# The slots of two weight rings moved from 8192 to 8208 bytes apart

## The chip, the cores and the metric

The kernel runs on one core of one Trainium2 chip. The metric is the device time of one execution in microseconds (us). Three runs of the kernel before gave 1250.34, 1250.72 and 1251.28 us; the median is 1250.72 us.

## What is computed

The reference is one transformer stack in float32 on 256 tokens of width 1024: first two layers (a gated delta-rule mixer with 8 heads, then block attention with 8 heads, each followed by a squared-ReLU MLP of width 4096), then a third layer with four parallel branches (differential attention, forgetting attention, a 31-tap convolution, a short convolution), a gated sum of them, cross attention to 256 memory tokens and a gated feed-forward of width 2816. For this case only one thing matters: nearly all of the work is a product of activations with a weight matrix that is read once from memory.

```python
h = h + squared_relu_mlp(rmsnorm(h, mlp_norm_g[i]), mlp_w_up[i], mlp_w_down[i])
def squared_relu_mlp(hn, w_up, w_down):
    return jnp.square(jax.nn.relu(hn @ w_up)) @ w_down
```

## The kernel before

The weights come in units of 1 MB: 128 partitions by 2048 float32, so 8192 bytes in each partition. SyncE starts one DMA for each unit into one of the two slots of `raw` (line 285). ScalarE rounds the unit into a slot of the ring `whi` (line 297: the high part, type fp32r), and VectorE writes what the rounding left into the same slot of the ring `wlo` (line 305: raw minus high). Both rings have four slots (`RING = 4`), and unit U lies in slot U mod 4. The splits run three units ahead of the product (`AHEAD = 3`).

TensorE then multiplies. The activations are split the same way: `xparts` holds the high and low halves of the 256 normed tokens (turned, 8 pieces of 256 columns each), `hhi` and `hlo` the hidden values of an MLP, `bhi` and `blo` the outputs of attention and of the branches. Every product is high*high + high*low + low*high, so a weight tile is used by three matmuls (`mm3`, lines 369, 372 and 373). There are four forms of it:

- features (line 426 on): the weights are the stationary operand, tiles of 128x128 of `whi` or `wlo`; `xparts` or `bhi`/`blo` stream past, 256 columns. 48 matmuls for each unit.
- tokens (line 577 on): activations are stationary, `whi` or `wlo` streams, 256 columns. 48 matmuls.
- rows (line 592 on): `hhi`/`hlo` (or `bhi`/`blo`, or `xparts`) are stationary, `whi` or `wlo` streams, 512 columns. 24 matmuls; the down projections.
- wide (line 441 on): `wlo` is stationary and the high half of `xparts` streams, 256 columns (line 450), then `whi` is stationary and both halves of `xparts` stream in one matmul of 512 columns (line 454). 32 matmuls; the up projections of the MLPs.

Each matmul has its own load of the stationary operand (PEld in the profile), which runs while the matmul before it streams. So at every moment TensorE reads two things from the memory on the chip: the moving operand of one matmul and the stationary operand of the next, and of the two one lies in a ring of weights and the other in a buffer of activations.

Buffers stand in a partition in the order in which `build` makes them (lines 167 to 199): `raw` (16384 bytes), `whi` (32768), `wlo` (32768), `xparts` (16384), `hhi` and `hlo` (4096 each), `h`, `gain` (8192 each), `smr`, `ident`, `ones` (512 each), `row_of` (64), `staged_rows`, `row_parts` (1024 each), `upper` (512), `masks` (3072), `dn_lower` (512), `smo` (256), `sm` (1024), `common` (39392), `head_rows`, `dn_x` (2048 each), and then `bhi` and `blo` (16384 each), over the place of `dn_extra`, which is given back before. All of them up to `common` are multiples of 64 bytes; `common` is not (39392 = 615 * 64 + 32). So seen from the start of any slot of `whi` or `wlo`, `xparts`, `hhi` and `hlo` lie at a whole number of 64 bytes, and `bhi` and `blo` lie 32 bytes past one (from `whi`: 159008 = 2484 * 64 + 32).

Of the kernel before, what the change touches and what calls it, by code (L numbers as in the profile page):

```python
# [22 lines left out]
F32R = mybir.dt.float32r  # L23
# [5 lines left out]
P = 128  # L29
# [4 lines left out]
RING = 4  # L34
RAW = 2
AHEAD = 3
UNIT = 2048
# [119 lines left out]
def build(nc, A, out):  # L157
    ctx = ExitStack()
    with ctx:
        def sb(name, shape, dt=F32, c=ctx):  # L160
            return c.enter_context(nc.sbuf_tensor(name, shape, dt))
# [3 lines left out]


        raw = sb("raw", [P, RAW, UNIT])
        whi = sb("whi", [P, RING, UNIT], F32R)
        wlo = sb("wlo", [P, RING, UNIT], F32R)
        xparts = sb("xparts", [P, 2, KT, T], F32R)  # L170
        xhi, xlo = xparts[:, 0], xparts[:, 1]
        hhi = sb("hhi", [P, 2, 2, T], F32R)
# [3453 lines left out]
```

## Time and profile before

| | |
|---|---|
| median of 3 runs | 1250.72 us |
| span of the profiled execution | 1249.1 us |
| granted TensorE clock over the span | 0.998 of 2.4 GHz |
| PE busy | 1220.7 us (98%) |
| PEld busy | 1106.9 us (89%) |
| DVE busy | 871.6 us (70%) |
| ACT busy | 700.5 us (56%) |
| weights split (L297, L305) | 190 units each |

The span runs from the first to the last instruction of the profiled execution; it is 1.6 us shorter than the median of the timed runs. PE is TensorE's matmuls, PEld its loads of the stationary operand, DVE VectorE, ACT ScalarE. Matmuls are pipelined and overlap in the records, so what one costs in a long sequence is not its duration but its pitch: the distance from its start to the start of the next.

### The profile page before, as it was taken

What the parts mean: (1) busy time and instruction counts of PE and PEld (TensorE: products, weight loads), DVE (VectorE), ACT (ScalarE), POOL (GpSimd) and SP (SyncE); (2) the same over time, 40 slices, a digit from 0 to 9 for tenths busy, and PEclk for the clock granted to TensorE, in tenths of its full rate; (3) what the DMA queues carried; (4) which work ended last, traced back from release to release, by engine and by line L of the source; (5) the groups of instructions that cost most, each with busy time, mean ns of one, the idle gap of its engine ahead of it and who ended that gap; (6) DMA issues with size and microseconds to landing.
All of it is one profiled execution on the core that took longest, in us unless ns stands there. A gap on an engine that the chain in (4) does not pass through costs nothing.

```text
span 1249.1 us, 21521 instructions
## 1 busy us (share of the span) xinstructions
PE 1220.7 (98%) x8583; PEld 1106.9 (89%) x8583; DVE 871.6 (70%) x1252; ACT 700.5 (56%) x1016; POOL 56.3 (5%) x102
## 2 busy tenths in 40 slices
PE   8999989999999999999999999999999999999997
PEld 7999988888888998888888999999999977888886
DVE  5888567666666656666656589998656577778876
ACT  4984555555455554554554564656454456666663
POOL 5010020000000001000000000000000010000000
PEclk9999999999999999999999999999999999999999
DMA  7671134666554654565555565354546534555561
GB/s 223 197 203 68 38 122 150 222 214 202 186 184 151 203 165 141 166 211 180 184 185 167 172 210 184 118 162 145 179 150 203 186 107 147 174 194 190 201 201 68
DMA packets 160340, 210.80 MB, mean 169 GB/s; under 512 B 5542, under 2 KB 143220, under 8 KB 160261
## 3 DMA queue, kind: packets, MB, share of 16 engines
q1 hardware_dynamic: 157315, 202.77, 50.6%
q0 software_dynamic: 1904, 6.85, 1.4%
q8 instruction: 57, 0.93, 0.3%
q10 hardware_dynamic: 1042, 0.07, 0.1%
q14 instruction: 22, 0.18, 0.0%
HBM read 208.62 MB, written 1.05 MB: 168 GB/s over the span
## 4 chain that ended last, share of the span: by engine, by line
PE 79%; DVE 10%; ACT 4%; issue 2%; DMA 2%; SPq 1%; POOL 1%; DVEq 0%; POOLq 0%; ACTq 0%
PE bank L369 16%; PE bank L373 16%; PE bank L372 16%; PE bank L454 15%; PE bank L450 8%; DVE wlo L305 3%; ACT whi L297 2%; PE bank L1425 2%; DMA raw<-in_dn_w_in 1%; DVE common L2582 1%; PE bank L2003 1%; PE bank L1445 1%; ACT common L753 1%; SPq L3388 1%; PE bank L2095 1%
## 5 line engine op out<-in xcount | busy, mean ns | idle before, releaser
L305 DVE TENSOR_TENSOR wlo<-raw,whi 128x2048 fp32r<-128x2048 f32 x190 | 434.9, 2291 | 203.6 <-ACT whi L297 203.3
L297 ACT ACTIVATE whi<-raw 128x2048 fp32r<-128x2048 f32 x190 | 363.3, 1913 | 145.4 <-PE bank L369 43.5
L369 PE MATMUL bank<-xparts,whi 128*128 128x256 f32 x912 | 262.5, 288 | 0.4 <-DVE common L2764 0.4
L373 PE MATMUL bank<-xparts,wlo 128*128 128x256 f32 x912 | 258.7, 284 | 0.0
L372 PE MATMUL bank<-xparts,whi 128*128 128x256 f32 x912 | 258.6, 284 | 0.0
L454 PE MATMUL bank<-xparts,whi 128*128 128x512 f32 x832 | 208.0, 392 | 0.0
L369 PEld LDWEIGHTS bank<-xparts,whi 128*128 128x128 f32 x912 | 175.5, 192 | 2.8 <-issue 2.1
L372 PEld LDWEIGHTS bank<-xparts,whi 128*128 128x128 f32 x912 | 175.6, 192 | 0.6 <-issue 0.5
L373 PEld LDWEIGHTS bank<-xparts,wlo 128*128 128x128 f32 x912 | 175.5, 192 | 0.0
L454 PEld LDWEIGHTS bank<-xparts,whi 128*128 128x128 f32 x832 | 149.8, 189 | 26.9
L369 PE MATMUL bank<-whi,hhi 128*128 128x512 f32 x392 | 153.1, 391 | 3.8 <-DVE hlo L1061 2.3
L372 PE MATMUL bank<-wlo,hhi 128*128 128x512 f32 x392 | 152.6, 389 | 0.0
L373 PE MATMUL bank<-whi,hlo 128*128 128x512 f32 x392 | 152.6, 389 | 0.0
L450 PEld LDWEIGHTS bank<-xparts,wlo 128*128 128x128 f32 x832 | 112.9, 190 | 8.7 <-DVE wlo L305 0.7
L450 PE MATMUL bank<-xparts,wlo 128*128 128x256 f32 x832 | 115.9, 283 | 0.7 <-DVE wlo L305 0.4
L369 PEld LDWEIGHTS bank<-whi,hhi 128*128 128x128 f32 x392 | 73.6, 188 | 20.8 <-issue 4.1
L373 PEld LDWEIGHTS bank<-whi,hlo 128*128 128x128 f32 x392 | 73.6, 188 | 15.4
L372 PEld LDWEIGHTS bank<-wlo,hhi 128*128 128x128 f32 x392 | 73.6, 188 | 15.0
L493 ACT ACTIVATE common<-bank 128x256 f32<-128x256 f32 x104 | 37.1, 377 | 75.5 <-PE bank L454 75.4
L506 DVE TENSOR_TENSOR common<-bank,common 128x256 f32<-128x256 f32 x104 | 41.3, 420 | 42.5 <-ACT common L493 42.5
L2582 DVE SCALAR_TENSOR_TENSOR common<-common,fc 128x256 f32<-128x256 f32 x120 | 49.5, 483 | 0.0
L1958 ACT ACTIVATE common<-bank 128x512 f32<-128x512 f32 x30 | 17.9, 596 | 50.5 <-PE bank L373 49.8
(391 smaller groups left out, 1706.2 us busy)
## 6 DMA issues: line engine op xcount, KB each, us to landing
raw<-in_mlp_w_up SPq DMA_DIRECT2D x32, 1024.0 KB, 5.5
raw<-in_mlp_w_down SPq DMA_DIRECT2D x32, 1024.0 KB, 5.1
raw<-in_w_in SPq DMA_DIRECT2D x22, 1024.0 KB, 5.3
raw<-in_w_up SPq DMA_DIRECT2D x22, 1024.0 KB, 5.2
raw<-in_w_gate SPq DMA_DIRECT2D x16, 1024.0 KB, 5.5
raw<-in_dn_w_in SPq DMA_DIRECT2D x15, 1024.0 KB, 5.8
raw<-in_mb_w_in SPq DMA_DIRECT2D x12, 1024.0 KB, 5.2
raw<-in_w_down SPq DMA_DIRECT2D x11, 1024.0 KB, 4.9
```

What stands on the lines that cost most here:

```text
L297: nc.scalar.activation(whi[:, s, :], raw[:, r, :], ACT.Copy).then_inc(hi_ready, 1)
L305: nc.vector.tensor_tensor(wlo[:, s, :], raw[:, V % RAW, :], f32(whi[:, s, :]), ALU.subtract).then_inc(lo_ready, 1)
L369: ins = pe.matmul(o, shi, mhi, start=first, stop=False, skip_group_check=True)
L372: pe.matmul(o, shi, mlo, start=False, stop=False, skip_group_check=True)
L373: return pe.matmul(o, slo, mhi, start=False, stop=last, skip_group_check=True)
L450: return pe.matmul(uses[f].ps[:, 0:T], wl[:, k, f * P:(f + 1) * P], xhi[:, k, :], start=start, stop=False, skip_group_check=True)
L454: return pe.matmul(wide_sums(uses[f]), wh[:, k, f * P:(f + 1) * P], xparts[:, :, k, :], start=False, stop=stop, skip_group_check=True)
L493: nc.scalar.activation(dst[:, f * T:(f + 1) * T], uses[f].ps[:, T:2 * T], ACT.Copy)\
L506: nc.vector.tensor_tensor(part, uses[f].ps[:, 0:T], part, ALU.add).then_inc(uses[f].freed, 1)
L1425: ins = pe.matmul(blk(use, hd), lhs(hd), rhs(hd), start=(hd == 0), stop=(hd == 3), skip_group_check=True)
L1958: nc.scalar.activation(b.dst, b.use.ps[:, :], ACT.Copy, scale=b.scale).then_inc(b.use.freed, 1)
L2582: ins = nc.vector.scalar_tensor_tensor(conv_y[:, f, :], src, dw_w[:, j, f:f + 1], conv_y[:, f, :], ALU.mult, ALU.add)
```

## The change

The two rings get rows of `UNIT + 4` elements, and the names `whi` and `wlo` become views of the first `UNIT` elements of each row. Everything that uses them is the same. A slot now starts 8208 = 8192 + 16 bytes after the one before. `wlo` starts 64 bytes later than before, and `xparts` and everything behind it 128 bytes later; `raw` stays.

```diff
         raw = sb("raw", [P, RAW, UNIT])
-        whi = sb("whi", [P, RING, UNIT], F32R)
-        wlo = sb("wlo", [P, RING, UNIT], F32R)
+        hi_slots = sb("whi", [P, RING, UNIT + 4], F32R)
+        lo_slots = sb("wlo", [P, RING, UNIT + 4], F32R)
+        whi, wlo = hi_slots[:, :, 0:UNIT], lo_slots[:, :, 0:UNIT]
         xparts = sb("xparts", [P, 2, KT, T], F32R)
```

## Rows read from the trace of the kernel before

**Rows 1.** The page, part 1: busy time of each engine over the span.

```profile
PE 1220.7 (98%) x8583; PEld 1106.9 (89%) x8583; DVE 871.6 (70%) x1252; ACT 700.5 (56%) x1016; POOL 56.3 (5%) x102
```

**Rows 2.** The page, part 4: the chain that ended last, by engine and by line.

```profile
PE 79%; DVE 10%; ACT 4%; issue 2%; DMA 2%; SPq 1%; POOL 1%; DVEq 0%; POOLq 0%; ACTq 0%
PE bank L369 16%; PE bank L373 16%; PE bank L372 16%; PE bank L454 15%; PE bank L450 8%; DVE wlo L305 3%; ACT whi L297 2%; PE bank L1425 2%; DMA raw<-in_dn_w_in 1%; DVE common L2582 1%; PE bank L2003 1%; PE bank L1445 1%; ACT common L753 1%; SPq L3388 1%; PE bank L2095 1%
```

**Rows 3.** Groups by line and shape: count, busy us, mean ns (out<-moving,stationary for PE).

```profile
L305 DVE TENSOR_TENSOR wlo<-raw,whi 128x2048 fp32r<-128x2048 f32 x190 | 434.9, 2291 | 203.6 <-ACT whi L297 203.3
L297 ACT ACTIVATE whi<-raw 128x2048 fp32r<-128x2048 f32 x190 | 363.3, 1913 | 145.4 <-PE bank L369 43.5 <-PE bank L450 26.8 <-DMA raw<-in_mlp_w_up 18.5
L369 PE MATMUL bank<-xparts,whi 128*128 128x256 f32 x912 | 262.5, 288 | 0.4 <-DVE common L2764 0.4
...
L454 PE MATMUL bank<-xparts,whi 128*128 128x512 f32 x832 | 208.0, 392 | 0.0
...
L369 PE MATMUL bank<-whi,hhi 128*128 128x512 f32 x392 | 153.1, 391 | 3.8 <-DVE hlo L1061 2.3 <-DVE hlo L2884 0.8 <-DVE hlo L3152 0.7
...
L450 PE MATMUL bank<-xparts,wlo 128*128 128x256 f32 x832 | 115.9, 283 | 0.7 <-DVE wlo L305 0.4 <-ACT xparts L826 0.2
...
L369 PE MATMUL bank<-bhi,whi 128*128 128x256 f32 x160 | 45.0, 281 | 0.0
...
L369 PE MATMUL bank<-whi,xparts 128*128 128x256 f32 x128 | 36.8, 288 | 0.0
...
L1061 DVE TENSOR_TENSOR hlo<-common,hhi 128x512 fp32r<-128x512 f32 x32 | 22.2, 693 | 1.4
...
L1050 ACT ACTIVATE hhi<-common 128x512 fp32r<-128x512 f32 x32 | 20.3, 635 | 1.0
...
L372 PE MATMUL bank<-wlo,bhi 128*128 128x512 f32 x48 | 19.0, 396 | 0.0
```

**Rows 4.** Timeline of PE from 308.3 us, rows form: start us, duration us, instruction.

```profile
308.33 0.39 PE L369 MATMUL bank<-whi,hhi 128*128 128x512 f32 x1
...
313.77 0.40 PE L450 MATMUL bank<-xparts,wlo 128*128 128x256 f32 x2
```

**Rows 5.** Timeline of PE from 313.5 us, wide form, eight matmuls to a line.

```profile
313.77 1.11 PE L450 MATMUL bank<-xparts,wlo 128*128 128x256 f32 x8
314.72 2.00 PE L454 MATMUL bank<-xparts,whi 128*128 128x512 f32 x8
316.56 1.11 PE L450 MATMUL bank<-xparts,wlo 128*128 128x256 f32 x8
```

**Rows 6.** Timeline of PE from 488.3 us, rows form with `bhi` and `blo` stationary.

```profile
488.42 0.40 PE L369 MATMUL bank<-whi,bhi 128*128 128x512 f32 x1
...
493.32 0.40 PE L369 MATMUL bank<-whi,bhi 128*128 128x512 f32 x1
```

**Rows 7.** Timeline of PE from 848.0 us, features form with `xparts` moving.

```profile
848.05 0.28 PE L372 MATMUL bank<-xparts,whi 128*128 128x256 f32 x1
...
850.93 0.28 PE L372 MATMUL bank<-xparts,whi 128*128 128x256 f32 x1
```

**Rows 8.** Timeline of PE from 961.0 us, features form with `bhi` and `blo` moving.

```profile
960.80 0.28 PE L369 MATMUL bank<-bhi,whi 128*128 128x256 f32 x1
...
962.90 0.28 PE L369 MATMUL bank<-xparts,whi 128*128 128x256 f32 x1
```

**Rows 9.** Timeline of PE from 682.5 us, tokens form with `bhi` and `blo` stationary.

```profile
682.48 0.28 PE L369 MATMUL bank<-whi,bhi 128*128 128x256 f32 x1
...
685.32 0.28 PE L369 MATMUL bank<-whi,bhi 128*128 128x256 f32 x1
```

**Rows 10.** Timeline of PE from 1235.5 us, rows form, just after a wait.

```profile
1235.34 0.40 PE L372 MATMUL bank<-wlo,hhi 128*128 128x512 f32 x1
...
1236.97 0.40 PE L373 MATMUL bank<-whi,hlo 128*128 128x512 f32 x1
...
1238.79 0.39 PE L372 MATMUL bank<-wlo,hhi 128*128 128x512 f32 x1
```

## The prediction, made before the changed kernel was run

> **What bounds the kernel now.** I read the page first. TensorE is busy 98% of the span [rows 1], and the chain that ended last is 79% matmuls, 71% of the span on the five lines that multiply with weights (16 + 16 + 16 + 15 + 8) [rows 2]; the two splits L305 and L297 hold 5% of it. So time is the number of weight matmuls times their pitch, plus some 5% in which the splits end last. The granted clock is 1.00 nearly throughout (the level of 2.4 GHz), and the change does nothing that would lower it.
>
> The change adds and removes no instruction, no byte of DMA and no wait. It can act only through addresses. So I then asked the trace whether any duration or pitch depends on an address.
>
> **The splits.** VectorE takes 2291 ns for 2048 elements at L305 and 693 ns for 512 at L1061: (2291 - 693) / 1536 = 1.04 ns for each further element. ScalarE takes 1913 ns and 635 ns (L297, L1050): (1913 - 635) / 1536 = 0.83 ns [rows 3]. The operands of L1061 and L1050 lie in other buffers at other distances, and one constant rate each fits both sizes: 1.04 * 512 = 533 and 0.83 * 512 = 426, so some 160 and 209 ns stand fixed in each instruction. I see nothing that a better distance could take out. A loss is possible if a start that is only a multiple of 16 bytes costs a little: I take zero, and as the other end 1% of the 5% of the chain, 0.6 us, which is small beside what follows. SyncE's DMAs write into `raw`, which does not move.
>
> **The matmuls: what an address does.** The trace has the same two forms at two distances. Between rings and `xparts`, `hhi`, `hlo` the distance is a whole number of 64 bytes; between rings and `bhi`, `blo` it is 32 bytes more.
>
> - 512 columns, distance 0: 24 matmuls from 308.33 to 313.77 us, 5.44 / 24 = 226.7 ns [rows 4]. Distance 32: 21 matmuls from 488.42 to 493.32 us, 4.90 / 21 = 233.3 ns [rows 6]. Worse by 6.6 ns.
> - 256 columns, weights stationary, distance 0: 24 matmuls in 2.88 us, 120.0 ns [rows 7]. Distance 32: 18 matmuls from 960.80 to 962.90 us, 116.7 ns [rows 8]. Better by 3.3 ns.
> - 256 columns, weights moving, distance 32: 24 matmuls in 2.84 us, 118.3 ns [rows 9]; better by 1.7 ns than the 120.0 of distance 0.
> - wide form: the eight matmuls of L454 take 316.56 - 314.72 = 1.84 us, 230.0 ns each, the eight of L450 0.95 us, 118.8 ns each [rows 5]; both include a start in which the pitch is not yet settled.
>
> The mean durations say the same: 396 ns against 391 for 512 columns, 281 against 288 for 256 [rows 3]. And the pitch is no function of the addresses alone: right after a wait, at unchanged distance, seven matmuls took 1.63 us (232.9 ns) and the next eight 1.82 us (227.5 ns) [rows 10]. I read this as two streams, the moving operand and the next stationary one, that get in each other's way now and then, and settle into a rhythm that the distance selects. The 512-column form sits in the shortest rhythm that these rows show; the 256-column form doesn't.
>
> The Trainium skill says otherwise: the page "TensorE: Matmul & The Clock Gate", Part 2, "Step-by-step", has "Loading the next tile's weights doesn't steal SBUF read bandwidth from the running matmul", and "SBUF — State Buffer", section "Who interferes with whom", gives PE two independent read ports and lets it wait for nobody. By that rule the pitch would be blind to distance and the sum zero. Rows 4 and 6, 6.6 ns apart for one form, do not bear it out.
>
> **What the change does to the distances.** Slot s starts 16 s bytes further into its 64 bytes; `wlo` moves by 64 and the activations by 128. If what counts is the distance within 64 bytes, slot 0 keeps its 0, slots 1, 2, 3 get 16, 32, 48. Only 32 is priced by a row. `bhi` and `blo` go to 32 less 16 s: slot 2 becomes 0, a quarter of 480 + 144 matmuls, under 0.5 us and of both signs, left out.
>
> **The sum.** Units go round the four slots, so three of four matmuls change. I price 16 and 48 like 32, the nearest row.
>
> - 256 columns, weights stationary: 3 * 912 + 832 = 3568 matmuls (L369, L450 [rows 3]; each of L372 and L373 has L369's count), 0.75 * 3568 * -3.3 ns = -8.8 us.
> - 256 columns, weights moving: 3 * 128 = 384; 0.75 * 384 * -1.7 = -0.5 us.
> - 512 columns, `hhi`/`hlo` stationary: 3 * 392 = 1176; 0.75 * 1176 * 6.6 = +5.8 us.
> - 512 columns of the wide form: 832, today 230.0 ns; at 233.3 it loses 3.3: 0.75 * 832 * 3.3 = +2.1 us.
>
> Together -9.3 + 7.9 = -1.4 us. Their pitches add up to 3952 * 0.120 + 1176 * 0.2267 + 832 * 0.230 = 932 us, with the `bhi` forms (480 * 0.117 + 144 * 0.233) 1022 us, of which the chain has 71% of 1249.1 = 887 us: 0.87 of a change shows, -1.2 us. The profiled execution would go from a span of 1249.1 to 1247.9 us, the median, 1.6 us above the span, from 1250.7 to 1249.5 us.
>
> Bounds. Below: 256 columns cost 120.0 and 512 cost 226.7, so a column costs 106.7 / 256 = 0.417 ns and 13.3 ns are left in each matmul; were all of it the streams' quarrel and gone in three slots, 0.75 * 5960 * 13.3 = 59 us would go, 1191 us. No row is near that. Above: 512 columns at 6.6 ns more and 256 columns no better gives +7.9 * 0.87 = 7 us; if 16 and 48 are twice as bad as 32, some 12 us, 1263 us.
>
> **The rivals.**
>
> 1. Distance doesn't matter, and `bhi` differs for another reason; equally, that the settled rhythm is kept whatever the slot. For: the skill's rule above, and the settled pitches are the same from unit to unit. Against: rows 6, 8 and 9, three forms with one thing in common. It gives 1250.7 us. Chance 0.17.
> 2. Faster: the 256-column forms gain as with 32, and the 512-column forms keep 226.7 in slots 1 and 3, or the gain of 256 is larger at 16 and 48. For: the 512-column pitch of 226.7 has been reached from several starts [rows 4, 10]. Against: the only other distance has lost it. -9.3 * 0.87 = -8 us: 1242.6 us. Chance 0.25.
> 3. Slower: every unit now has another distance than the one before, so the rhythm has to settle anew in each. In rows 10 seven matmuls of 512 columns lost 7 * (232.9 - 226.7) = 43 ns in settling. There are 2736 / 48 = 57 units of features, 832 / 16 = 52 wide and 1176 / 24 = 49 of rows. If the 512-column forms pay 233 in all three moved slots and the 256-column ones get stuck at 120, it is +7.9 * 0.87 = +7 us: 1257.6 us. It decides from the point where 256 columns gain less than 2.7 ns (7.9 us over 0.75 * 3952 matmuls). Chance 0.25.
>
> The forecast has 0.33: both effects are there and nearly cancel, 1246 to 1253 us.
>
> **How the numbers follow.** The predicted time is 1249.5 us. About 0.2%, 2.5 us, is what a measurement of this kernel tells from no change. The forecast gives 0.08 faster, 0.22 same, 0.03 slower; with the rivals (0.17 same, 0.25 faster, 0.25 slower) that is 0.33 faster, 0.39 same, 0.28 slower. The unknown price of the distances 16 and 48 (two of three moved slots) makes the range: with 3 ns either way on 2000 matmuls of 256 and 1000 of 512 columns it is some 8 us each side, and I put 1239 to 1260 us.
>
> **What the profile after would show.** In a stretch of rows form the pitch should go in fours, one unit at 226.7 ns and three near 233; in features 120.0 in one slot and under 118 in three. The mean of L369 `whi,hhi` should rise from 391 ns, that of L369 `xparts,whi` fall from 288. MLP stretches should be longer, projections into heads and gates shorter. L305 and L297 should stay within 10 ns. I am wrong if the means of all forms move the same way, if slot 0 moves as well (then more than 64 bytes count), or if the splits move.

## The result: 0.2% slower, and each form moved as its sign was forecast

| | before | changed |
|---|---|---|
| median of 20 runs each, us | 1251.49 | 1254.07 |
| ratio of the times | | 1.0021 (95%: 1.0013 to 1.0029) |
| span of the profiled execution, us | 1249.1 | 1251.1 |

The change costs 2.6 us (1.6 to 3.6 by the interval); I had forecast 1.2 us less, inside what I called the same. The page of the changed kernel (one line was added, so line numbers are one higher from 168 on), first its parts 1 and 4:

```profile
PE 1222.9 (98%) x8583; PEld 1100.7 (88%) x8583; DVE 871.2 (70%) x1252; ACT 700.1 (56%) x1016; POOL 58.3 (5%) x102
...
PE 77%; DVE 11%; ACT 5%; issue 3%; DMA 2%; SPq 1%; POOL 1%; DVEq 0%; POOLq 0%; ACTq 0%
```

Against [rows 1] little seems to have happened: a busy time is the time covered by at least one record, and those of PE, DVE and ACT stay within 0.2%; PEld's fell by 0.6%. The chain [rows 2] has a little less PE and a little more DVE, ACT and issue. The groups by line show the change, in opposite directions (count | busy us, mean ns):

```profile
L306 DVE TENSOR_TENSOR wlo<-raw,whi 128x2048 fp32r<-128x2048 f32 x190 | 434.7, 2289 | 201.7 <-ACT whi L298 201.4
L298 ACT ACTIVATE whi<-raw 128x2048 fp32r<-128x2048 f32 x190 | 363.7, 1915 | 146.6 <-PE bank L370 44.2
L370 PE MATMUL bank<-xparts,whi 128*128 128x256 f32 x912 | 260.2, 285 | 0.4 <-DVE common L2765 0.4
...
L455 PE MATMUL bank<-xparts,whi 128*128 128x512 f32 x832 | 209.7, 394 | 0.0
...
L370 PE MATMUL bank<-whi,hhi 128*128 128x512 f32 x392 | 154.8, 395 | 3.3 <-DVE hlo L1062 1.7
...
L451 PE MATMUL bank<-xparts,wlo 128*128 128x256 f32 x832 | 114.4, 280 | 0.7 <-ACT xparts L827 0.7
```

Against [rows 3]: matmuls of 256 columns went from 288 to 285 and from 283 to 280 ns, those of 512 columns from 391 to 395 and from 392 to 394. The splits stand still, 2291 to 2289 and 1913 to 1915 ns, although their slots now start at every multiple of 16 bytes.

Where the time went is read from the starts of the same six groups of eight matmuls in both timelines of PE (start us, duration us); the kernel before:

```profile
225.56 1.12 PE L450 MATMUL bank<-xparts,wlo 128*128 128x256 f32 x8
368.90 1.11 PE L450 MATMUL bank<-xparts,wlo 128*128 128x256 f32 x8
509.48 1.12 PE L450 MATMUL bank<-xparts,wlo 128*128 128x256 f32 x8
663.85 1.12 PE L450 MATMUL bank<-xparts,wlo 128*128 128x256 f32 x8
1067.65 1.19 PE L450 MATMUL bank<-xparts,wlo 128*128 128x256 f32 x8
1220.04 1.11 PE L450 MATMUL bank<-xparts,wlo 128*128 128x256 f32 x8
```

and the changed kernel:

```profile
224.64 1.11 PE L451 MATMUL bank<-xparts,wlo 128*128 128x256 f32 x8
370.00 1.10 PE L451 MATMUL bank<-xparts,wlo 128*128 128x256 f32 x8
510.10 1.11 PE L451 MATMUL bank<-xparts,wlo 128*128 128x256 f32 x8
666.39 1.10 PE L451 MATMUL bank<-xparts,wlo 128*128 128x256 f32 x8
1068.23 1.19 PE L451 MATMUL bank<-xparts,wlo 128*128 128x256 f32 x8
1221.87 1.10 PE L451 MATMUL bank<-xparts,wlo 128*128 128x256 f32 x8
```

| stretch | before, us | changed, us | difference |
|---|---|---|---|
| start to the first MLP | 225.56 | 224.64 | -0.92 |
| first MLP | 143.34 | 145.36 | +2.02 |
| attention layer | 140.58 | 140.10 | -0.48 |
| second MLP | 154.37 | 156.29 | +1.92 |
| third layer up to its feed-forward | 403.80 | 401.84 | -1.96 |
| feed-forward | 152.39 | 153.64 | +1.25 |

The names are rough: each border is one shown group near the first or the last up projection, so one or two units of an MLP lie in the stretch beside it, and the third layer has some 512-column matmuls too. The stretches that are mostly 512-column matmuls lost 5.2 us, the others won 3.4 us back. But my account of the slots was wrong, as four rows of the second MLP show (PE timeline of the changed kernel; the unit from 515.67 us lies in slot 0, the one from 526.82 us in slot 2):

```profile
515.67 0.39 PE L370 MATMUL bank<-whi,hhi 128*128 128x512 f32 x1
...
520.52 0.39 PE L370 MATMUL bank<-whi,hhi 128*128 128x512 f32 x1
...
526.82 0.40 PE L370 MATMUL bank<-whi,hhi 128*128 128x512 f32 x1
...
531.73 0.40 PE L370 MATMUL bank<-whi,hhi 128*128 128x512 f32 x1
```

In each pair lie 21 matmuls: 4.85 / 21 = 231.0 ns in slot 0, 4.91 / 21 = 233.8 ns in slot 2. Slot 0, whose distance I had called unchanged, has left 226.7 ns as well.

### The profile page after: what moved, and what is told of

Same layout as the page of the kernel before. It is cut to its first block, busy times and chain, and to the rows that moved or that the text cites. A ratio compares the mean times of both kernels' runs of the same rounds, so it can differ in the third digit from the quotient of the medians.

```text
span 1251.1 us, 21521 instructions
## 1 busy us (share of the span) xinstructions
PE 1222.9 (98%) x8583; PEld 1100.7 (88%) x8583; DVE 871.2 (70%) x1252; ACT 700.1 (56%) x1016; POOL 58.3 (5%) x102
## 4 chain that ended last, share of the span: by engine, by line
PE 77%; DVE 11%; ACT 5%; issue 3%; DMA 2%; SPq 1%; POOL 1%; DVEq 0%; POOLq 0%; ACTq 0%
PE bank L370 16%; PE bank L374 16%; PE bank L373 16%; PE bank L455 15%; PE bank L451 8%; DVE wlo L306 4%; ACT whi L298 2%; PE bank L1426 2%; DVE common L2583 1%; DMA raw<-in_dn_w_in 1%; PE bank L1446 1%; ACT common L754 1%; SPq L3389 1%; PE bank L2004 1%; POOL nrs L767 1%
## 5 line engine op out<-in xcount | busy, mean ns | idle before, releaser
L306 DVE TENSOR_TENSOR wlo<-raw,whi 128x2048 fp32r<-128x2048 f32 x190 | 434.7, 2289 | 201.7 <-ACT whi L298 201.4
L298 ACT ACTIVATE whi<-raw 128x2048 fp32r<-128x2048 f32 x190 | 363.7, 1915 | 146.6 <-PE bank L370 44.2
L370 PEld LDWEIGHTS bank<-xparts,whi 128*128 128x128 f32 x912 | 172.2, 189 | 2.8 <-issue 2.5
L455 PEld LDWEIGHTS bank<-xparts,whi 128*128 128x128 f32 x832 | 149.1, 188 | 28.0
L373 PEld LDWEIGHTS bank<-xparts,whi 128*128 128x128 f32 x912 | 172.0, 189 | 0.7 <-issue 0.5
L374 PEld LDWEIGHTS bank<-xparts,wlo 128*128 128x128 f32 x912 | 172.0, 189 | 0.0
L451 PEld LDWEIGHTS bank<-xparts,wlo 128*128 128x128 f32 x832 | 111.7, 188 | 9.7 <-DVE wlo L306 0.7
L370 PE MATMUL bank<-bhi,whi 128*128 128x256 f32 x160 | 45.0, 281 | 0.0
```

Source lines behind the costliest of these rows:

```text
L298: nc.scalar.activation(whi[:, s, :], raw[:, r, :], ACT.Copy).then_inc(hi_ready, 1)
L306: nc.vector.tensor_tensor(wlo[:, s, :], raw[:, V % RAW, :], f32(whi[:, s, :]), ALU.subtract).then_inc(lo_ready, 1)
L370: ins = pe.matmul(o, shi, mhi, start=first, stop=False, skip_group_check=True)
L373: pe.matmul(o, shi, mlo, start=False, stop=False, skip_group_check=True)
L374: return pe.matmul(o, slo, mhi, start=False, stop=last, skip_group_check=True)
L451: return pe.matmul(uses[f].ps[:, 0:T], wl[:, k, f * P:(f + 1) * P], xhi[:, k, :], start=start, stop=False, skip_group_check=True)
```

## The experiments

My theory after the result: a pitch follows the distance between ring and activations, and more than the low six bits of it count. The rivals: only the slots' 16 bytes act, and slot 0 inherits the rhythm of the unit before; or the starts of the buffers act by themselves. In all runs but one the slots are 8192 bytes apart again, so in each of them every unit has the same distance. The table gives the mean pitch of each form (distance from start to start, in unbroken sequences of the profiled execution; features is `xparts` over `whi`/`wlo`, with L450) and the ratio of the times to the kernel before on the same chip.

| run | features, 256 | wide L454, 512 | rows, 512 | time / before (95%) |
|---|---|---|---|---|
| before | 119.8 | 230.0 | 226.9 | 1 |
| changed kernel | 118.2 | 232.1 | 232.2 | 1.0021 (1.0013 to 1.0029) |
| e1_starts_only | 117.4 | 232.1 | 231.1 | 1.0004 (0.9995 to 1.0014) |
| e2_all16 | 117.4 | 231.8 | 232.2 | 1.0011 (1.0000 to 1.0022) |
| e3_x32 | 116.9 | 233.0 | 232.7 | 1.0024 (1.0014 to 1.0033) |
| e4_x16 | 117.4 | 232.0 | 232.3 | 1.0005 (0.9994 to 1.0016) |
| e5_gap256 | 119.7 | 230.1 | 226.9 | one execution, 1251.1 us |
| e6_gap512 | 119.7 | 230.1 | 227.0 | one execution, 1252.7 us |
| e7_x128_h512 | 118.8 | 232.7 | 227.7 | 1.0006 (0.9996 to 1.0016) |
| e8_x32_h256 | 116.9 | 233.3 | 227.7 | 0.9972 (0.9959 to 0.9985) |
| e9_x16_h256 | 117.7 | 231.8 | 227.7 | 0.9972 (0.9963 to 0.9981) |
| e10_slots_only | 118.5 | 230.8 | 231.2 | 1.0006 (0.9996 to 1.0016) |
| e11_h32_only | 119.6 | 230.3 | 233.1 | 1.0038 (1.0023 to 1.0053) |
| e12_x240_h256 | 117.3 | 233.1 | 227.8 | 0.9973 (0.9959 to 0.9986) |

### The starts without the slots

```diff
         whi = sb("whi", [P, RING, UNIT], F32R)
+        gap_a = sb("gap_a", [P, 16])
         wlo = sb("wlo", [P, RING, UNIT], F32R)
+        gap_b = sb("gap_b", [P, 16])
```

> Slots stay 8192 bytes apart; only the starts of the buffers move as in the changed kernel (wlo by 64 bytes, xparts and everything behind by 128). If only the distance within 64 bytes counts, every pitch stays as before: rows form 227 ns (mean duration of L369 whi,hhi 391 ns), features 120.0 ns (288), and the time is 1251 us. If distances of 64 and 128 bytes count too, the rows form goes to some 231 ns in all slots, as slot 0 of the changed kernel shows, features to some 118.6 ns, and the time moves by at most 3 us either way.

The second case came: 231.1 ns in rows, 117.4 in features, with no slot moved at all. So the 64 and 128 bytes by which the starts moved do by themselves most of what the changed kernel does to the pitches, and the low six bits are not all that counts.

### Prices of 16 and 32 bytes

All activations 16 bytes past a multiple of 64 (`hlo` in the same way as `hhi`); for the other two runs only `xparts`, by 32 and by 16 bytes:

```diff
-        xparts = sb("xparts", [P, 2, KT, T], F32R)
-        hhi = sb("hhi", [P, 2, 2, T], F32R)
+        xparts = sb("xparts", [P, 2 * KT * T + 32], F32R)[:, 4:4 + 2 * KT * T].rearrange(
+            "p (a k t) -> p a k t", a=2, k=KT)
+        hhi = sb("hhi", [P, 4 * T + 32], F32R)[:, 4:4 + 4 * T].rearrange("p (a b t) -> p a b t", a=2, b=2)
```

> Slots stay 8192 bytes apart; xparts, hhi and hlo all start 16 bytes past a multiple of 64 bytes as seen from the rings, in every unit alike. This prices the distance 16, which no row of before shows. Theory (the pitch follows the distance within 64 bytes and 16 costs like 32): rows form 233 ns, features 117 ns, wide form's L454 233 ns, time within 2 us of before. Rival (16 is worse than 32 for 512 columns or no better for 256): rows form 234 ns or more, features 119 to 120 ns, time 1255 to 1260 us.

> Slots stay 8192 bytes apart; only xparts moves by 32 bytes, hhi and hlo stay at a multiple of 64 bytes from the rings. Theory: features fall from 120.0 to 116.7 ns (912 x 3 matmuls) and L450 likewise, L454 loses some 3 ns, rows form keeps 226.7 ns: 3568 x -3.3 + 832 x 3.3 = -9.0 us, 0.87 of it shows, 1243.5 us. Rival (the pitch of bhi's matmuls comes from something else than its distance): nothing moves, 1251 us.

> As the run with xparts moved by 32 bytes, but by 16. If 16 is priced like 32: features 117 ns and 1243.5 us. If the gain needs 32 bytes: features 119 to 120 ns, L454 231 to 233 ns, 1250 to 1253 us.

Features and L454 came as the theory said, but rows went to 232.3 and 232.7 ns where I had said that they would keep 226.7. The padding explains it: it moved `hhi` by 128 bytes, which I had taken for no move (in e2_all16 `hhi` lies 144 and `hlo` 272 bytes further, not 16). So 128 bytes change rows about as much as 32 do, 64 and 128 change features about as much as 16, and what needs an explanation is the kernel before: it stands at a special distance. For the two runs that moved `xparts` alone the times fell short of the expectation by 11 and 8 us. The loss in rows took most of the gain in features; that doesn't explain all of it, as said below.

### The period of the special distance

```diff
+        gap = sb("gap", [P, 64])
         xparts = sb("xparts", [P, 2, KT, T], F32R)
```

(`[P, 128]` in the run with 512 bytes.)

> Slots 8192 bytes apart, rings unmoved, a gap of 256 bytes ahead of xparts, so xparts and everything behind it lies 256 bytes further from the rings. Shifts of 16, 32, 64 and 128 bytes all changed the pitches alike, so the old state is one special distance. If it repeats every 256 bytes: rows form 226.9 ns, features 119.8 ns (mean durations of L369 391 and 288 ns) as before. If it repeats only every 512 bytes or more: rows 231 to 233 ns, features 117 to 118 ns.

> The same with a gap of 512 bytes. In the features form the two column halves of a unit already lie 512 bytes apart and both show 120 ns, so a distance of 512 should be equal to none: rows 226.9 ns, features 119.8 ns. If even this changes them (rows 231 ns or more), the start of a buffer itself counts and not its distance, or a period above 512 does.

The groups by line with a gap of 256 bytes:

```profile
L370 PE MATMUL bank<-xparts,whi 128*128 128x256 f32 x912 | 262.5, 288 | 0.4 <-DVE common L2765 0.4
...
L455 PE MATMUL bank<-xparts,whi 128*128 128x512 f32 x832 | 208.0, 392 | 0.0
L370 PE MATMUL bank<-whi,hhi 128*128 128x512 f32 x392 | 153.1, 391 | 3.7 <-DVE hlo L1062 2.2 <-DVE hlo L2885 0.8 <-DVE hlo L3153 0.7
```

and with the starts moved by 64 and 128 bytes (the same groups, line numbers one higher):

```profile
L371 PE MATMUL bank<-xparts,whi 128*128 128x256 f32 x912 | 259.5, 285 | 0.4 <-DVE common L2766 0.4
...
L456 PE MATMUL bank<-xparts,whi 128*128 128x512 f32 x832 | 209.7, 394 | 0.0
...
L371 PE MATMUL bank<-whi,hhi 128*128 128x512 f32 x392 | 153.6, 392 | 3.6 <-DVE hlo L1063 1.8 <-DVE hlo L3154 0.9 <-DVE hlo L2886 0.7
```

With 256 bytes even the busy times of [rows 3] come back to the tenth of a microsecond (262.5, 208.0, 153.1), and with 512 bytes the pitches do as well, in one execution each. So the pattern repeats after 256 bytes, and not after 128. In the kernel before every ring, `xparts`, `hhi` and `hlo` start at the same place within 256 bytes, since all sizes between them are multiples of 4096.

### Each form by itself

`hhi` and `hlo` moved by 32 bytes, nothing else off the special distance:

> Slots 8192 bytes apart, xparts unmoved, hhi and hlo 32 bytes past a multiple of 256 bytes from the rings, everything behind at a multiple of 256. Theory: only the rows form changes, 226.9 to 232.7 ns, 1162 x 5.8 = +6.7 us; features keep 119.8 and L454 230.0 ns; 1256 to 1258 us. Rival (the pitches of one form depend on the other buffers): features or L454 move as well.

```profile
L369 PE MATMUL bank<-xparts,whi 128*128 128x256 f32 x912 | 261.8, 287 | 0.4 <-DVE common L2764 0.4
...
L454 PE MATMUL bank<-xparts,whi 128*128 128x512 f32 x832 | 208.2, 392 | 0.0
L369 PE MATMUL bank<-whi,hhi 128*128 128x512 f32 x392 | 155.4, 396 | 3.6 <-DVE hlo L1061 2.0 <-DVE hlo L2884 0.7 <-DVE hlo L3152 0.7
```

Only rows moved (391 to 396 ns; 226.9 to 233.1 in pitch), and 1.0038, 4.8 us, is the price of the 512-column form alone; the rival, that forms depend on other forms' buffers, falls for this run. The pitch sum is 1176 * 6.2 = 7.3 us, so about two thirds of it (0.66) reached the time; with four timed runs the interval of the ratio allows 2.9 to 6.6 us, 0.40 to 0.91.

### The slots without the starts

```diff
-        whi = sb("whi", [P, RING, UNIT], F32R)
-        wlo = sb("wlo", [P, RING, UNIT], F32R)
+        hi_slots = sb("whi", [P, RING, UNIT + 4], F32R)
+        gap_a = sb("gap_a", [P, 48])
+        lo_slots = sb("wlo", [P, RING, UNIT + 4], F32R)
+        gap_b = sb("gap_b", [P, 48])
+        whi, wlo = hi_slots[:, :, 0:UNIT], lo_slots[:, :, 0:UNIT]
```

> The changed kernel's slots, 8208 bytes apart, but 192 bytes of gap behind each ring, so wlo, xparts and everything behind start at a multiple of 256 bytes from whi. Theory: slot 0 is back at the old special distance and shows 226.9 ns in the rows form and 119.8 ns in features, slots 1, 2 and 3 (16, 32, 48 bytes) show 232 to 233 ns and 117 to 118 ns; so a bit under three quarters of the loss in rows and of the gain in features, time 1251 to 1254 us. Rival (a unit inherits the rhythm of the one before it): slot 0 too shows over 228 ns in rows.

The same two units as above, slot 0 and slot 2, in the timeline of this run, with the wide unit between them (slot 1):

```profile
515.34 0.39 PE L372 MATMUL bank<-whi,hhi 128*128 128x512 f32 x1
...
520.11 0.39 PE L372 MATMUL bank<-whi,hhi 128*128 128x512 f32 x1
...
521.74 1.98 PE L457 MATMUL bank<-xparts,whi 128*128 128x512 f32 x8
523.55 1.11 PE L453 MATMUL bank<-xparts,wlo 128*128 128x256 f32 x8
...
526.31 0.40 PE L372 MATMUL bank<-whi,hhi 128*128 128x512 f32 x1
...
531.21 0.40 PE L372 MATMUL bank<-whi,hhi 128*128 128x512 f32 x1
```

4.77 / 21 = 227.1 ns in slot 0, 4.90 / 21 = 233.3 ns in slot 2. Mean pitches by slot, over all units:

| | slot 0 | slot 1 | slot 2 | slot 3 |
|---|---|---|---|---|
| rows, changed kernel | 231.3 | 233.0 | 233.8 | 231.1 |
| rows, slots only | 227.6 | 231.5 | 233.4 | 233.0 |
| L454, changed kernel | 232.1 | 233.0 | 233.0 | 230.4 |
| L454, slots only | 230.1 | 226.9 | 233.1 | 232.8 |

With the starts at a multiple of 256 bytes, slot 0 is back at the old pitch. So it was not a neighbour's rhythm that moved slot 0 in the changed kernel, but the 128 bytes of the starts. The time is 1.0006, not told from no change: three slots pay, one doesn't.

This run also settles whether each operand's own start counts, and not the distance between the two. In it `bhi` and `blo` still lie 32 bytes past a multiple of 256, and slot 2 does too: both operands are off the old place, and their distance is zero. The unit of rows form that reads them there:

```profile
476.63 0.39 PE L372 MATMUL bank<-whi,bhi 128*128 128x512 f32 x1
...
479.35 0.39 PE L372 MATMUL bank<-whi,bhi 128*128 128x512 f32 x1
```

2.72 / 12 = 226.7 ns, where the same unit of the kernel before shows 233.3. The 256-column forms go with it: the settled pitch of the unit in slot 2 at 873 us, with `bhi` moving, is 119.9 ns (117.8 before), of the one at 682 us, with the weights moving, 120.0 (118.3 before). So it is the distance that selects the pitch.

### A better layout

`xparts` off the special distance, where features gain, and `hhi`/`hlo` kept at it, where rows are at their best:

```diff
-        xparts = sb("xparts", [P, 2, KT, T], F32R)
+        xparts = sb("xparts", [P, 2 * KT * T + 64], F32R)[:, 8:8 + 2 * KT * T].rearrange(
+            "p (a k t) -> p a k t", a=2, k=KT)
```

The first attempt used 128 bytes for `xparts` and 512 for the rest (offset 32, padding 128 elements), before the period was known; then 32, 16 and 240 bytes with 256 (offsets 8, 4 and 60, padding 64).

> xparts lies 128 bytes, hhi and hlo (and everything behind) 512 bytes further from the rings. Theory (a period of 512 or 256 bytes, each form follows its own pair of buffers): features 117.4 ns as with all starts moved, rows keep 226.9 ns, L454 230 to 232 ns: 3640 x -2.4 + 830 x 2 = -7 us, 1244 to 1245 us, faster than both kernels. Rival (pitches of rows change whenever anything does): rows 231 to 233 ns, 1251 to 1253 us.

> Slots 8192 bytes apart. xparts 32 bytes further from the rings, hhi, hlo and everything behind 256 bytes further, a distance that proved equal to none. Theory (period of 256 bytes, each form follows the distance of its own two buffers): features 116.9 ns and L454 233.0 ns as in the run with xparts moved by 32 bytes, rows form back at 226.9 ns: 3640 x -2.8 + 830 x 3.0 = -7.7 us of pitch, 0.87 of it in the time: 1244 to 1246 us against 1251. Rival (a gain in pitch does not reach the time, since the splits or transfers then end last): pitches as said, time 1249 to 1251 us.

> The same with 16 bytes in place of 32: features 117.4 ns, L454 232.0 ns, rows 226.9 ns: -8.7 + 1.6 = -7.1 us of pitch, 1244.5 to 1246.5 us; by the rival 1249 to 1251 us.

> Slots 8192 bytes apart, xparts 240 bytes further from the rings, hhi, hlo and everything behind 256. By the period of 256 bytes that is a distance of minus 16, the one that slot 1 has in the run with moved slots only, where L454 showed 226.9 ns in place of 230.0 and features fell by 1.4 ns. Theory (the sign of the distance matters, and a slot's pitch belongs to its distance alone): L454 226.9 ns, features 118.4 ns, rows 227 ns: -1.4 x 3640 - 3.1 x 830 = -7.7 us of pitch, 1246 to 1249 us. Rival (minus 16 is like plus 16, and slot 1's value came from its neighbours): L454 231.8 ns, features 117.7 ns, also near 1248 us.

128 bytes gave only 1.0 ns in features and lost 2.7 in L454: no gain. 32, 16 and 240 bytes give 0.9972, 0.9972 and 0.9973, medians of 1248.4, 1248.3 and 1248.4 us, faster than the kernel before, and so, by the two ratios, than the changed one; the pitches are near what was expected, and the time gains some 3.5 us, where for 32 and 16 bytes I had said 4.5 to 7. The groups by line of the run with 32 bytes:

```profile
L370 PE MATMUL bank<-xparts,whi 128*128 128x256 f32 x912 | 259.4, 284 | 0.4 <-DVE common L2765 0.4
...
L455 PE MATMUL bank<-xparts,whi 128*128 128x512 f32 x832 | 210.5, 395 | 0.0
L370 PE MATMUL bank<-whi,hhi 128*128 128x512 f32 x392 | 153.4, 391 | 3.6 <-DVE hlo L1062 1.9 <-DVE hlo L3153 0.9 <-DVE hlo L2885 0.9
```

284 against 288 for features, 395 against 392 for L454, 391 kept for rows. The pitch of rows is 227.7 and not 226.9 ns because each unit now has to settle after the wide unit ahead of it: in the unit at 512.76 us of this run the first six matmuls take 231.7 ns each and the next fifteen 226.7. It is a price like the one of [rows 10], some 22 ns a unit.

The last run missed in one point: at the distance at which L454 had shown 226.9 ns in slot 1 of e10_slots_only, it shows 233.1 here. But its own first wide unit of the second MLP, where sixteen of L454 follow one another, shows the other value (the lines at 520.89 us are of a later unit):

```profile
505.23 3.79 PE L455 MATMUL bank<-xparts,whi 128*128 128x512 f32 x16
508.86 1.10 PE L451 MATMUL bank<-xparts,wlo 128*128 128x256 f32 x8
...
520.89 2.02 PE L455 MATMUL bank<-xparts,whi 128*128 128x512 f32 x8
522.75 1.10 PE L451 MATMUL bank<-xparts,wlo 128*128 128x256 f32 x8
```

3.63 / 16 = 226.9 ns against 1.86 / 8 = 232.5. A pitch therefore doesn't belong to the distance alone; for one distance there is more than one settled rhythm. Even the kernel before has two, for `bhi` moving at distance 32. [rows 8] is from a unit in slot 0 that follows a unit of rows form; another unit in slot 0, which follows features:

```profile
934.66 0.28 PE L369 MATMUL bank<-bhi,whi 128*128 128x256 f32 x1
...
937.49 0.28 PE L369 MATMUL bank<-bhi,whi 128*128 128x256 f32 x1
```

2.83 / 24 = 117.9 ns, against the 116.7 of [rows 8]. Of the ten units of this kind eight settle at 117.8 ns, and the two that show 116.7 are the two that start right behind a unit of rows form. So which rhythm is reached depends on what ran before.

### What the pitches don't explain

The spans of single executions differ by more than the pitches do. Part of it is the granted clock. The kernel before and the run with only the starts moved, in four stretches (us, busy us of PE, PEld, DVE, ACT, POOL, clock, DMA share, GB/s); before:

```profile
140.00:150.00 10.00, 10.00 (x103) 9.93 (x101) 5.89 (x20) 5.41 (x16) 0.00 (x0) 1.00 0.01 2
...
168.00:180.00 12.00, 11.40 (x60) 10.18 (x61) 9.45 (x25) 6.17 (x7) 1.20 (x2) 0.86 0.49 176
```

starts only:

```profile
140.00:150.00 10.00, 10.00 (x88) 9.91 (x86) 5.99 (x20) 4.91 (x15) 0.00 (x0) 0.83 0.01 2
...
168.00:180.00 12.00, 9.60 (x57) 8.17 (x58) 10.17 (x28) 5.19 (x7) 1.20 (x2) 1.00 0.50 176
```

Short of the very end, each has one stretch of 3.4 us at the lower level (1.2 GHz), but at another place: from 170.0 us, among features, in the one, and from 141.4 us, among small matmuls, in the other, where 88 matmuls start in 10 us in place of 103. Right behind it the second case is 1.6 us later (the same weight unit starts at 145.67 us, before at 144.06); once the kernel before has had its own stretch, 0.5 us of that are left (174.70 against 174.19). The changed kernel has it near 170 us, like the kernel before (0.86 in the same stretch), so it is no part of their difference. Why one place or the other is granted was not tried. Nor do the pitches give the times: by the working of the table further down the first four runs sum to -2.2, -1.3, -1.6 and -1.1 us, and their times went by +0.5, +1.4, +3.0 and +0.6 us. The time of e3_x32 is explained least: its pitches sum to about the same as those of e4_x16, its ratio is 1.0024 against 1.0005; one execution of each shows the clock's step at different places, but whether that holds for the timed runs can't be seen.

## Why the prediction was wrong, step by step

**The bound** was right: TensorE's pitch is what the change moves, and the splits stayed within 2 ns. **"At 32 bytes the 512-column form loses 6.6 ns and the 256-column form wins"** was right in sign for every form, and in size where every unit has that distance: 226.9 to 233.1 ns for rows when `hhi` and `hlo` alone moved, 116.9 ns for features when `xparts` did. The first rival, that distance doesn't matter, has fallen: in e11_h32_only two buffers moved by 32 bytes cost 4.8 us. The Trainium skill's rule that stood beside it ("TensorE: Matmul & The Clock Gate", Part 2, "Step-by-step: what each phase is for": the load of the next weights takes no read bandwidth from the running matmul) does not tell this pitch, which the place of the stationary operand alone moved by 6.2 ns. By what means the two reads get in each other's way no run shows; the streams' quarrel stays a reading.

**"If what counts is the distance within 64 bytes, slot 0 keeps its 0"** is the step of the mechanism that failed. The period is 256 bytes (e5_gap256, e6_gap512), the starts of `wlo` and the activations moved by 64 and 128, so four slots of four left the special distance and not three. The prediction has both numbers, 64 and 128, and reduces them modulo 64 for no better reason than that `bhi` was the one counter-example and is off by 32. It is 32 modulo 256 as well; no row told the two apart, and the bounds should have held both.

**The terms of the sum**, with what they measured (mean pitch difference times count):

| term | forecast, us | measured, us |
|---|---|---|
| features and L450 | -8.8 | 3568 * -1.6 = -5.7 |
| weights moving, 256 | -0.5 | 384 * -0.6 = -0.2 |
| rows, 512 | +5.8 | 1176 * 5.3 = +6.2 |
| L454 | +2.1 | 832 * 2.1 = +1.7 |
| sum | -1.4 | +2.0 |

The 512-column terms were right within 0.4 us each: three slots at 6.6 or four at 5.3 are nearly the same sum, which is luck. The term that was mis-sized, and that gave the sum its wrong sign, is features: 3.1 of the 3.4 us between the two sums. **"0.75 * 3568 * -3.3 ns"**, the gain of [rows 8] at a steady 116.7 ns in each of three slots, 16 and 48 bytes priced like 32, is the step that failed there. In the changed kernel (features units with `xparts`, from the tenth matmul on) slot 2 keeps the old rhythm in every unit:

```profile
738.47 0.28 PE L370 MATMUL bank<-xparts,whi 128*128 128x256 f32 x1
...
742.79 0.28 PE L370 MATMUL bank<-xparts,whi 128*128 128x256 f32 x1
...
744.21 0.28 PE L370 MATMUL bank<-xparts,whi 128*128 128x256 f32 x1
...
748.42 0.28 PE L370 MATMUL bank<-xparts,whi 128*128 128x256 f32 x1
```

4.32 / 36 = 120.0 ns in slot 2, 4.21 / 36 = 116.9 ns in slot 3; slot 1 shows 118.5 in nearly all units, and slot 0 anything from 115.6 to 120.0. With features at 117.4, as at the starts' distance alone, the sum would have been -0.9 us. The rows of before held a warning: the 116.7 of [rows 8] is the faster of two values for the same slot and buffers, and with the 117.8 of the other eight units the term would have been 0.75 * 3568 * -2.2 = -5.9 us and the sum +1.5.

**"0.87 of a change shows"**, one factor for both signs, was wrong too, though not for the changed kernel, where 0.87 * 2.0 = 1.7 us lies inside the 1.6 to 3.6 us measured. In e8_x32_h256 losses of 3.6 us and gains of 10.8 us sum to -7.2 us of pitch, and the time went by 3.5 us (1.9 to 5.1), 0.26 to 0.71 of it; and in the first four runs the sum fell and the time did not. A reading that fits: of the loss in rows 0.66 came through (e11_h32_only, 0.40 to 0.91); if that holds elsewhere, 0.66 * 7.9 = 5.2 us of the changed kernel's loss came through, and of its gain of 5.9 only 5.2 - 2.6 = 2.6 us, 0.44. In e8_x32_h256 the same working gives 0.66 * 3.6 = 2.4 us of loss against 5.9 of 10.8 us of gain, 0.55. That gains come through less than losses fits the chain, where DVE, ACT and issue have 19% in the changed kernel and in e8_x32_h256, against 16% before and 17% in e11_h32_only, where nothing became faster: where the projections stand, splits and small steps are next in line. It is a reading with wide intervals and not shown by itself.

**The rivals.** The third, that units settle anew and 256 columns get stuck at 120, had the right sign and was right in part. For rows it was not the cause: e1_starts_only shows 231.1 ns with the same distance in every unit. For features it was near: slot 2 is stuck at 120.0 ns, and in e10_slots_only slot 1 shows a settled 118.4 ns at a distance of minus 16 that gives 117.1 where every unit has it (e12_x240_h256). The second, fast features and rows kept, is what the changed kernel did not do and what the layout with two distances does.

## What to carry to other kernels

When a kernel is bound by matmuls, compare the pitch of one form across buffers: if it differs, addresses, or what runs just before, are part of the cost, and padding one buffer is a tuning step with a sign for each form. Price a move of addresses by every buffer that it shifts, those behind it included, and test the period with one gap before reasoning in remainders. A padding that moves one group of operands and restores the rest (here 32 and 256 bytes) can keep the gain without the loss; the slot distance can't, because it puts every unit at another distance.

## What the runs showed of the hardware

For matmuls of fp32r with a load of the stationary operand each, the pitch depends on the distance between moving and stationary operand within 256 bytes: at a distance of zero 119.8 ns for 256 and 226.9 ns for 512 columns (rows form), elsewhere on the mean of a run 117 to 119 and 231 to 233 ns. By these means zero is the best place for the rows form and the worst for 256 columns; for L454, whose mean at zero is 230.0 ns, slot 1 of e10_slots_only was better (226.9). Several settled rhythms exist at one distance (226.9 or 233.1 ns for L454, 116.7 or 117.8 ns for `bhi`), and what ran before chooses among them. VectorE and ScalarE showed nothing of the kind: the mean durations of the two splits stayed within 2 and 4 ns over all runs (2291 and 1913 ns before), at all distances and, in the two runs with moved slots, with slots at every multiple of 16 bytes.
